# GpSimd multiplies the rows by the norm's weights, DVE scales by the factor of the row

## What is computed

```python
def rmsnorm(x, g):
    xf = x.astype(jnp.float32)
    r = lax.rsqrt(jnp.mean(xf * xf, axis=-1, keepdims=True) + EPS)
    return (xf * r).astype(x.dtype) * g

def merge_heads(o_fox, o_nsa, g, w_out):
    o = jnp.concatenate([rmsnorm(o_fox, g[:FOX_W]), rmsnorm(o_nsa, g[FOX_W:])], axis=-1)
    return o @ w_out
```

## Time and profile before

| | us |
|---|---|
| median of 3 runs | 2427.74 |
| lowest and highest | 2425.32, 2428.02 |
| the profiled execution, whole | 2427.58 |
| its span, first to last instruction | 2425.9 |
| granted TensorE clock, mean | 0.904 of full |
| busy: PE, DVE, ACT, POOL | 2027.9, 1022.3, 818.8, 382.8 |

### The profile page before, as it was taken

How to read it: one execution, slowest core, us unless ns; L and a number is a source line. 1 busy time by engine, 2 the same in 40 slices (tenths; PEclk the granted TensorE clock), 3 DMA queues, 4 the chain that set the end, 5 groups by cost and what they waited for, 6 DMA issues and landing times. The chain is left out here.

```text
span 2425.9 us, 36147 instructions
## 1 busy us (share of the span) xinstructions
PE 2027.9 (84%) x12288; PEld 1758.8 (73%) x12288; DVE 1022.3 (42%) x2106; ACT 818.8 (34%) x1565; POOL 382.8 (16%) x493
## 2 busy tenths in 40 slices
PE   5876879995465389999999669599999999799997
PEld 4775877785333178888888658389999999776664
DVE  4444323113232145766767641423333333355564
ACT  4544011212121015655666520322222222144454
POOL 2100012135030421212110000021221212000000
PEclk9887899997788558999999879699999999899999
DMA  5412536225863482222220032311111111221101
GB/s 140 91 49 81 191 130 216 85 97 162 256 204 112 116 154 66 53 53 59 55 59 0 11 121 81 111 49 40 52 40 46 52 35 52 102 77 61 35 26 46
DMA packets 170651, 210.02 MB, mean 87 GB/s; under 512 B 39804, under 2 KB 128181, under 8 KB 170407
## 3 DMA queue, kind: packets, MB, share of 16 engines
q1 hardware_dynamic: 145674, 133.28, 18.4%
q0 software_dynamic: 24864, 75.38, 11.0%
HBM read 173.63 MB, written 40.18 MB: 88 GB/s over the span
## 5 line engine op out<-in xcount | busy, mean ns | idle before, releaser
L118 PE MATMUL y_acc<-w_down_split_hi,act_split_hi 128*128 128x512 f32 (+1 forms) x396 | 163.7, 413 | 20.0 <-DVE act_split_lo L2572 18.0
L118 PE MATMUL gate_acc<-h_T_hi,w_gate_split_hi 128*128 128x352 f32 x528 | 172.3, 326 | 7.7 <-POOL w_gate_split_lo L2422 7.7
L118 PE MATMUL up_acc<-h_T_hi,w_up_split_hi 128*128 128x352 f32 x528 | 170.3, 323 | 0.0
L119 PE MATMUL gate_acc<-h_T_lo,w_gate_split_hi 128*128 128x352 f32 x528 | 170.2, 322 | 0.0
L120 PE MATMUL gate_acc<-h_T_hi,w_gate_split_lo 128*128 128x352 f32 x528 | 170.1, 322 | 0.0
L119 PE MATMUL up_acc<-h_T_lo,w_up_split_hi 128*128 128x352 f32 x528 | 169.2, 320 | 0.0
L120 PE MATMUL up_acc<-h_T_hi,w_up_split_lo 128*128 128x352 f32 x528 | 169.1, 320 | 0.0
L2120 ACT ACTIVATE pa_scores<-pa_scores,pa_neg_max 128x128 f32<-128x128 f32 (+1 forms) x192 | 144.1, 751 | 67.5 <-DVE pa_neg_max L2154 61.4
L2128 ACT ACTIVATE pa_probs_T_hi<-pa_t 128x512 fp32r<-128x512 f32 (+3 forms) x288 | 125.1, 469 | 107.4 <-PE pa_t L2082 106.1
L2183 DVE TENSOR_TENSOR pa_probs_T_lo<-pa_t,pa_probs_T_hi 128x512 fp32r<-128x512 f32 (+3 forms) x288 | 144.9, 531 | 32.7 <-ACT pa_probs_T_hi L2128 30.6
L119 PE MATMUL y_acc<-w_down_split_lo,act_split_hi 128*128 128x512 f32 (+1 forms) x396 | 156.7, 396 | 0.0
(11 more groups left out here) (400 smaller groups left out, 5001.5 us busy)
## 6 DMA issues: line engine op xcount, KB each, us to landing
fox_k_pages<-in_cache_fox_kv SPq DMA_DIRECT2D x64, 256.0 KB, 4.4
w_rows<-in_cache_fox_kv POOLq DMA_DIRECT2D x64, 256.0 KB, 4.6
w_gate<-in_w_gu SPq DMA_DIRECT2D x22, 512.0 KB, 3.8
w_up<-in_w_gu SPq DMA_DIRECT2D x22, 512.0 KB, 3.8
w_down_half<-in_w_down SPq DMA_DIRECT2D x22, 512.0 KB, 3.7
sel_pages<-in_cache_nsa_kv SPq DMA_DIRECT2D x64, 128.0 KB, 3.0
pa_k_fox<-scratch_kf_d POOLq DMA_DIRECT2D x32, 256.0 KB
w_rows<-in_w_in SPq DMA_DIRECT2D x3, 2048.0 KB, 15.8
```

The costliest lines, as they stand in the source:

```text
L118: pe.matmul(out, a[0][at], b[0][bt], start=start, stop=False)
L119: pe.matmul(out, a[0][at], b[1][bt], start=False, stop=False)
```

## The change

`norm_transpose` gets a tile `xg` with two buffers and a semaphore `s_xg`. GpSimd gets a list of nine instructions: it multiplies the rows of tile `t` by the weights into `xg`, when the rows and the weights are there and, from the third tile on, when DVE's multiply of tile `t - 2` has ended. DVE's instruction then has one tensor input, `xg`, and a scalar for each row, and it waits for `s_xg` in place of the weights. ScalarE, TensorE and SyncE keep their lists.

```diff
--- before.py
+++ after.py
@@ -135,6 +135,7 @@
         x = ph.sb(f"{name}_x", [P, 4, D]) if resident is None else ph.sb(f"{name}_x", [P, 1, D])
         xn = ph.sb(f"{name}_xn", [P, 2, D])
         sq = ph.sb(f"{name}_sq", [P, 2, D])
+        xg = ph.sb(f"{name}_xg", [P, 2, D])
         g = ph.sb(f"{name}_gain", [P, D])
         ss = ph.sb(f"{name}_ss", [P, 9, groups])
         ms = ph.sb(f"{name}_ms", [P, 9, groups])
@@ -148,6 +149,7 @@
         s_rt = ph.sem(f"{name}_root")
         s_rr = ph.sem(f"{name}_inverse")
         s_xn = ph.sem(f"{name}_normed")
+        s_xg = ph.sem(f"{name}_gained")
         s_tr = ph.sem(f"{name}_transposed")
         s_ev = ph.sem(f"{name}_copied")
         s_lo = ph.sem(f"{name}_rest_kept")
@@ -227,18 +229,28 @@
                 dve.wait_ge(s_rt, t + 1)
                 dve.reciprocal(rr[0:rows, t, :], rt[0:rows, t, :]).then_inc(s_rr, 1)
                 dve.wait_ge(s_rr, t + 1)
-                if t == 0:
-                    dve.wait_ge(s_g, 16)
+                dve.wait_ge(s_xg, t + 1)
                 if t >= 2:
                     dve.wait_ge(s_tr, t - 1)
                 for k in range(groups):
-                    ins = dve.scalar_tensor_tensor(
-                        out=xn[0:rows, t % 2, k * W:(k + 1) * W], in0=rows_of(t, slice(k * W, (k + 1) * W)),
-                        scalar=rr[0:rows, t, k:k + 1], in1=g[0:rows, k * W:(k + 1) * W], op0=ALU.mult, op1=ALU.mult)
+                    ins = dve.tensor_scalar(xn[0:rows, t % 2, k * W:(k + 1) * W], xg[0:rows, t % 2, k * W:(k + 1) * W],
+                                            rr[0:rows, t, k:k + 1], None, ALU.mult)
                 ins.then_inc(s_xn, 1)
                 if t >= 1:
                     rest(t - 1)
             rest(len(ROWS) - 1)
+
+        @block.gpsimd
+        def _(pool):
+            pool.wait_ge(s_g, 16)
+            for t, rows in enumerate(ROWS):
+                if resident is None:
+                    pool.wait_ge(s_x[t % 4], 16 * (t // 4 + 1))
+                elif t == NT:
+                    pool.wait_ge(s_x[t % 4], 16)
+                if t >= 2:
+                    pool.wait_ge(s_xn, t - 1)
+                pool.tensor_tensor(xg[0:rows, t % 2, :], rows_of(t, slice(0, D)), g[0:rows, :], ALU.mult).then_inc(s_xg, 1)
 
         @block.tensor
         def _(pe):
```

## The result

The changed kernel takes 2437.33 us (median of 6 runs, 2435.1 to 2438.79), the kernel before in the same comparison 2426.8 (2425.32 to 2430.28). The ratio is 1.0041, with a 95% interval of 1.0028 to 1.0054: slower by about 10 us. One execution in the whole study, of the changed kernel with another order on ScalarE, is left out of its median as slow: 2743.79 us at a granted clock of 0.753, where its others have 0.896 to 0.901.

What follows compares the result with a forecast made beforehand. The prediction took DVE's multiply, in a chain closing over two tiles at 2.9 us a tile, to bound the norms. Changes of 2.2 + 8.1 + 3.6 = +13.9 us on 2427.6 gave 2441.5 us, range 2432 to 2448.

Steps and rivals of the forecast that it cites:

- cycle, outer norms: First and last norm: GpSimd's multiply and DVE's take turns, 2.39 + (0.75 - 0.14) + 0.18 = 3.18 us a tile.
- cycle, middle norm: Middle norm: the two multiplies in turn, 3.31 us a tile, plus 0.30 for a mean that stands still.
- start, three norms: Tile 0 of each norm: DVE's multiply waits for two GpSimd multiplies; +0.4, +4.5 and +1.8 us.
- loop, three norms: From tile 0's multiply to the end of tile 7's, taking turns is slower: +1.8, +3.6 and +1.8 us.
- behind tile 7's multiply: End of each norm: transposes, copy and remainder are the same chain before and after, so nothing.
- the multiply's saving: DVE in the three norms: freed of 0.53 us a tile over 27 tiles, 14 us of busy time.
- the chain over two tiles: Norm loops before: 4.51 us beside the multiply's own 1.28, 5.79 for two tiles, 2.9 a tile.
- Standing still, and whose turn it is: Norms: DVE's new multiply stands still while GpSimd works, and GpSimd goes first each time; forecast case, chance 0.55.
- The means: DVE's mean: two columns in the middle norm stand still, 0.30 us a tile; one column elsewhere, nothing.
- (1): Norms: the engines overlap, DVE's multiply takes 0.75 us in the two-tile chain; total -5.0 us, 2422.6; chance 0.12.
- (2): Norms: DVE takes its turn after each single GpSimd multiply, so starts are cheaper; total +5.5 us, 2433.1; chance 0.15.
- (3): Norms: one-column means stand still too (+3.6 us) and GpSimd's multiply takes 2.56 (+4.1); total 2449 us; chance 0.18.

Runs made afterwards that it cites:

- the last experiment: Against the kernel before: GpSimd multiplies 512 columns, DVE the other 512 the old way, one-column means, new order on ScalarE; 2425.72 us, ratio 0.9992.

## Why the prediction was right, point by point

The forecast was 2441.5 us, in a range from 2432 to 2448; the time is 2437.33. Sign and mechanism are as forecast; the size was +13.9 against a measured +10.5 (+9.5 in the norms of the profiled execution). By its steps:

| | forecast | measured |
|---|---|---|
| new multiply; pair of 512 | 0.75; 0.88 | 0.75; 0.88 |
| GpSimd's multiply | 2.39 | 2.35 |
| held multiply's end behind GpSimd's | 0.61 | 0.55 |
| GpSimd's next start behind that | 0.18 | 0.14 |
| cycle, outer norms | 3.18 | 3.05 |
| cycle, middle norm | 3.61 | 3.44 |
| start, three norms | +0.4, +4.5, +1.8 | +0.2, +4.2, +1.5 |
| loop, three norms | +1.8, +3.6, +1.8 | +0.9, +2.4, +0.9 |
| behind tile 7's multiply | 0, 0, 0 | 0.0, -0.2, -0.5 |

The measured rows of the table are in the forecast's own stretches. The multiply of tile 0 ended 11.23, 5.75 and 9.89 us behind the norm's first issue, and now ends 10.92, 9.42 and 10.89 behind it; with the 0.53 by which it is shorter added, that is the start. From there to the end of tile 7's multiply it was 19.96, 20.86 and 19.95 us, and is 21.36, 23.83 and 21.37; less the 0.53, that is the loop.

**What bounds, and the multiply's saving.** Right in size: 0.75 was measured without the weights and with GpSimd one tile ahead, where nothing holds the multiply, and 0.88 in the middle norm of after. Wrong in one step, the path of the chain over two tiles. The prediction had it run through "ScalarE's square of a later tile, the root and DVE's reciprocal"; the runs with another order on ScalarE show that it runs through DVE's own remainder, which stands behind the copy, and ahead of the mean in DVE's list; in the middle norm the two paths tie within 0.1 us. The length (4.51 us) was read from the trace and did not hang on the path, and a shorter multiply shortens the one path as it does the other. So this did not move the forecast, only the idea of what else might help.

**Standing still, and whose turn it is.** Right, and it decided the sign. The multiply waits for GpSimd's end; at the start of each norm it waits for two multiplies of GpSimd; after that GpSimd is always first. The reason given, that the second multiply has begun before DVE hears of the first, is borne out by the start of the last experiment's middle norm, where DVE did not have to hear of it and got in between.

**The size of the cycle.** Here lie 3.0 of the 4.4 us by which the sum was too high. The outer cycle was 0.13 too long: 0.04 in GpSimd's multiply, for which the row of a subtraction was taken (2.39 against 2.35), 0.06 in the held multiply (taken to start 0.14 before GpSimd's recorded end, as a copy of four columns did; it starts some 0.20 before), 0.04 in the release of GpSimd, for which the one row of another pair of instructions gave an upper bound. Each is small, and seven tiles of three norms multiply them. In the middle norm they come to 7 x 3.44 against 7 x 3.61, nearly.

**Starts.** 0.7 too high together (6.0 against 6.7), for the same reasons, GpSimd's two multiplies first, and weights that landed 0.1 sooner than reckoned in the middle and the last norm.

**Behind tile 7.** Taken as nothing, and it was -0.7. In the first norm it is nothing (4.69 to 4.67); in the others it was longer before (4.91 and 5.12) and is 4.67 now. Before, tiles came 2.6 and 3.2 us apart in turn, and the norms ended in different places of that turn; the steady cycle of after has no such turn. No experiment was made for this, but the traces agree: in the outer norms of the old form, the stretch is 4.67 to 4.69 where the last multiply starts 2.5 to 2.7 behind the one before it, and 5.12 or 5.13 where it starts 3.15 behind.

**The means.** Right as taken: one column not held, two columns held. The run with two one-column means shows that the two-column form costs 1.8 us in the changed kernel. With ones in PSUM it costs 5.9 of the 6.0 us that the loop of the middle norm loses there (26.86 with it, 20.95 without, 20.86 in before).

**The rivals.** (1) The overlap did not happen; what it would have been worth is seen without GpSimd, where the norms lose 9.4 us. Against that stands the rival's 7.2, which has no wait at the start in it either: 7.6 are lost up to the end of tile 7's multiply, about as reckoned, and 1.7 behind it, where the rival had nothing. (2) DVE getting in between did not happen: the multiply of tile 0 ends behind the second one of GpSimd in all three norms. Its figure of 2433.1 is as near to the result as the forecast (4.2 below it, the forecast 4.2 above), but by chance: the forecast's terms were too large, and the turns were as forecast. (3) Neither of its parts came: the one-column means stay at 0.14 us, and GpSimd needs 2.35 and not 2.56.

## What to carry to other kernels

Work moved from DVE to GpSimd runs beside DVE only as far as DVE's own instructions there are of a kind that is not held. In this kernel those were the remainder and the multiply with one input in PSUM, the one-column mean and the reciprocal; held were the multiply with two inputs in SBUF and, of those with one, the tensor_scalar of two columns or more and the copy of four. For the held kinds the two times add. Here 2.35 + 0.55 + 0.14 had to be less than the 2.9 us of before, not the larger of 2.35 and 0.75. Look in the trace for the small instructions of DVE (a copy of four columns, a mean of two) that are sometimes ten times their shortest: they show who stands still, and their end minus their shortest length shows, to about 0.1 us, when the other engine really lets go. And where GpSimd's first results stand ahead of a chain, its start can cost more than the loop: here 4.2 of 6.4 us in the middle norm.

## What was not expected of the hardware

- The same tensor_scalar is not held at one column (0.13 to 0.15 us in all 18, 14 of which start inside a GpSimd multiply) and is at two (1.41 at the median), so that splitting an instruction in two made both together quicker, 0.21 against 1.41. A reciprocal of two columns is not held either, at 0.15.
- A held instruction takes over sooner than one that waits for the semaphore: it ends 0.55 behind GpSimd's recorded end, the other 0.84, with the same 0.75 of work. The cycles are 3.05 and 3.35.
- The old multiply with two inputs in SBUF is held as well, 2.28 against 1.28. With the second input in PSUM it is not, at 1.28. With the means by columns that frees the loops of DVE wholly beside GpSimd, at the price of the multiply's length.
- Two GpSimd multiplies issued back to back keep DVE out only if DVE comes late. Where its instruction was already held, it ran between the two, and GpSimd's pair took 2.93 in place of 2.52.
